# Convolving channel-major projection tiles beside the tile that follows, in a hybrid decoder step

## The chip, the cores and the metric

The kernel runs on one core of a Trainium2 chip. The time is device microseconds of that core, a median over runs. TensorE (PE, with its weight loads as PEld), VectorE (DVE), ScalarE (ACT), GpSimd (POOL) and SyncE (SP) each run one instruction stream in order and wait for each other through semaphores. DMAs are issued from SP, ACT and POOL; a "q" behind an engine's name in a row (SPq) is the engine's issue of one.

## The reference

One layer works on a prompt of 512 tokens and on 8 sequences of 4 new tokens (the sample, 32 rows), model width 2048. Everything starts from one projection; its first 5120 columns belong to the mLSTM mixer (2048 of q and k before the convolution, then 1024 each of v, output gate and group gate), the rest to sparse attention, its indexer and memory attention.

```python
(m_qk, m_v, m_o, m_gate, m_if, a_q, a_k, a_v, a_gate,
 i_q, i_w, i_k, c_q, c_gate) = split_in(rms_norm(x, g_pre) @ w_in)
qk, conv_state = causal_conv(m_qk, zeros, conv_w, conv_b)     # 4 taps over time, per channel, + bias, SiLU
m_out, (C, n, m) = mlstm_mixer(qk, m_v, m_o, m_if, b_if, head_norm, carry0, MLSTM_CHUNK)
```

`causal_conv` also returns the last three rows of `m_qk` (output `p_conv`). The mixer has 4 heads of 256 channels; each uses 256 channels of q and 256 of k. The sample has the same layer with its own states. At the end the three mixers' outputs are gated, joined, multiplied by `w_out`, normed and added to `x`.

## The kernel before

**Stages in order of time.** (1) Input rows are normed and turned, split into a high and a low FP32R part (`x_hi`, `x_lo`); (2) two tiles of memory keys and values; (3) the projection columns from 5120 up, for attention and the indexer; (4) ten tiles of 512 columns, n = `N_B0` to `N_Y0` - 1, which are columns 0 to 5119; the first four hold the 2048 columns that are convolved; (5) memory attention of the sample, with the gates of the mLSTM beside it (`beside_memory`); (6) the four mLSTM heads of the prompt, with the sample's mLSTM beside them (`beside_head`: preparation beside head 0, then 32 pairs of batch and head, 8 in each of heads 1 to 3 and 8 behind); (7) the output projection.

**A tile** (`tensor_tile`, L404 on) goes through 8 chunks of 256 rows of `w_in`. ACT casts a chunk to `w_hi` (L385), POOL subtracts to get `w_lo` (L389), both in two buffers. PE multiplies for each of four blocks of 128 tokens and for the sample rows: the tokens' `x` is the stationary operand and the 512 weight columns stream (L431 to L433; sample L426, L427), so a bank holds tokens by columns. At the tile's end ACT scales each bank by the tokens' `rstd` into `z_tile` (L471) and stores it to DRAM (`z_p`, L476).

**What is hosted.** Between chunks the streams carry pieces of other work, by generators that are stepped at fixed places: PE and ACT twice in a chunk, DVE two prompt steps and one step of `rows` per chunk. During the ten tiles this is the prompt's attention, block of 128 queries after block (`vector_prompt_prep`, L645; `vector_prompt_select`, L1184 to L1200, the scores added up and a top-k; `vector_prompt_attend`, L1275 to L1295), and the sample's sparse attention (physical addresses at L804 to L817, then one row after the other: POOL gathers, DVE multiplies and sums, L906 and L908). The order of the rows of each engine is thus written out in the program. POOL does a tile's `w_lo` and then one row's gather, and that waits until DVE has consumed the row two before.

**The heads.** SP loads for each head five blocks from `z_p`, two heads ahead: head h+2 after head h is through (`sync_mlstm_head`, L1534). q and k must be turned to channels by tokens: for each of 4 blocks of 128 channels of a head, PE turns (L1655, `tensor_conv_turn`), DVE runs four operations over 512 tokens from PSUM (L1667, L1669, `vector_conv`), ACT applies SiLU (L1681, `scalar_conv`). For head 0 this stands alone before the heads; for head h+1 one block stands in each of the four steps of head h. A step of a head is: DVE forms the decay's argument (L1764), ACT takes its exponential (L1849), PE multiplies keys by queries (L1709), DVE combines (L1769). Then PE sums over values (L1722, L1725), forms the new state (L1732, L1737), and DVE norms (L1780 to L1805). A pair of the sample is L2093, L2111, L2116 on PE, L2134 on ACT, L2145 and L2155 on DVE. The sample's preparation begins when SP has loaded its rows (L1921 to L1923; `vector_mlstm_s_prep`, L1965 on).

## Time and profile before

| | |
|---|---|
| median of 3 runs | 1880.14 us (1877.06 to 1888.46) |
| the profiled execution | 1877.01 us |
| its span | 1875.3 us |
| TensorE matmul busy | 1679.8 us (90%) |
| VectorE busy | 814.8 us (43%) |
| ScalarE busy | 569.1 us (30%) |
| GpSimd busy | 673.4 us (36%) |
| mean granted TensorE clock | 0.937 of full |

The profiled execution takes 1.7 us more than its span. Each busy time is a mean over all stages; the stages are read by windows of time. The ten tiles of stage 4 lie from about 567 to 1257 us, memory attention from 1257 to 1325, the heads from there to about 1600. Line numbers in rows are those of the kernel before.

### The profile page before, as it was taken

The page shows a single profiled execution, that of the slowest core. Times are in us where ns is not written, and L with a number is a line of the kernel's source. Part 1 is how long each engine was busy: PE and PEld are TensorE (multiplying, and loading weights), DVE is VectorE, ACT ScalarE, POOL GpSimd, SP SyncE. Part 2 cuts the span into 40 slices and gives each one's busy share as a digit, 9 for nine tenths or more (in the row PEclk, how much of TensorE's full clock was granted, in tenths as well). Part 3 has the DMA queues.
Part 4 walks back from the last instruction along what each step waited for, and adds up shares of the span by engine and source line. Part 5 has one row for each costly group of instructions (what it writes and reads, how often), then busy time and mean ns, then how long its engine had stood idle before and what let it go on. Part 6 is the DMA issues. An engine that isn't in the chain of part 4 may idle for free.

```text
span 1875.3 us, 20980 instructions
## 1 busy us (share of the span) xinstructions
PE 1679.8 (90%) x7801; PEld 1272.0 (68%) x7801; DVE 814.8 (43%) x1319; ACT 569.1 (30%) x876; POOL 673.4 (36%) x448
## 2 busy tenths in 40 slices
PE   6899999999999499998899999987658789799995
PEld 5677775677897376776688778865334455477774
DVE  6400010599929856755632161112465454501113
ACT  5522233222221233233222422224244443312221
POOL 3655531333333166766444444421110111033331
PEclk9999999999999699999999999998667788789997
DMA  6544431233344267766455544437404323542222
GB/s 214 160 134 130 142 101 56 71 105 108 92 120 144 77 196 231 221 197 211 122 154 165 149 134 117 147 125 230 93 29 152 107 68 107 192 160 85 83 78 106
DMA packets 139674, 249.01 MB, mean 133 GB/s; under 512 B 26504, under 2 KB 63308, under 8 KB 136296
## 3 DMA queue, kind: packets, MB, share of 16 engines
q10 hardware_dynamic: 66928, 122.86, 21.0%
q1 hardware_dynamic: 55920, 72.76, 12.2%
q0 software_dynamic: 16736, 52.18, 9.6%
q8 instruction: 58, 0.95, 0.2%
q14 instruction: 32, 0.26, 0.0%
HBM read 204.11 MB, written 43.66 MB: 132 GB/s over the span
## 4 chain that ended last, share of the span: by engine, by line
PE 73%; DVE 13%; DMA 5%; ACT 4%; issue 2%; POOL 1%; ACTq 1%; SPq 0%; DVEq 0%; POOLq 0%
PE acc L431 16%; PE acc L433 16%; PE acc L432 16%; PE acc L426 4%; PE acc L427 4%; PE ps_c L991 3%; PE acc L1722 2%; DVE arena L1669 1%; PE ps_c L2116 1%; PE acc L2111 1%; DMA arena<-z_prompt 1%; PE ps_a L1155 1%; POOL w_lo L389 1%; ACT z_tile L471 1%; PE ps_a L1224 1%
## 5 line engine op out<-in xcount | busy, mean ns | idle before, releaser
L389 POOL TENSOR_TENSOR w_lo<-w_raw,w_hi 128x1024 fp32r<-128x1024 f32 (+1 forms) x200 | 466.7, 2334 | 814.8 <-ACT w_hi L385 814.5
L431 PE MATMUL acc<-w_hi,x_hi 128*128 128x512 f32 (+1 forms) x1472 | 580.4, 394 | 8.8 <-DVE keep L925 5.3
L433 PE MATMUL acc<-w_hi,x_lo 128*128 128x512 f32 (+1 forms) x1472 | 565.9, 384 | 0.0
L432 PE MATMUL acc<-w_lo,x_hi 128*128 128x512 f32 (+1 forms) x1472 | 565.3, 384 | 0.0
L385 ACT CAST w_hi<-w_raw 128x1024 fp32r<-128x1024 f32 (+1 forms) x200 | 204.2, 1021 | 758.3 <-PE acc L427 716.6
L431 PEld LDWEIGHTS acc<-w_hi,x_hi 128*128 128x128 f32 x1472 | 278.8, 189 | 93.9 <-issue 28.0
L433 PEld LDWEIGHTS acc<-w_hi,x_lo 128*128 128x128 f32 x1472 | 278.1, 189 | 55.8
L432 PEld LDWEIGHTS acc<-w_lo,x_hi 128*128 128x128 f32 x1472 | 278.8, 189 | 51.4 <-issue 0.7
L426 PE MATMUL acc<-w_hi,x_hi 128*64 128x512 f32 (+1 forms) x368 | 141.4, 385 | 0.0
L427 PE MATMUL acc<-w_lo,x_hi 128*64 128x512 f32 (+1 forms) x368 | 140.9, 384 | 0.0
L2231 DVE TENSOR_TENSOR arena<-arena (+1 forms) x16 | 14.0, 887 | 176.8 <-ACT arena L464 176.8
L471 ACT ACTIVATE z_tile<-acc,small 128x512 f32<-128x512 f32 (+3 forms) x95 | 63.6, 669 | 48.3 <-PE acc L433 32.1
L881 POOL DMA_INDIRECT arena<-in_cache_attn_k,keep x64 | 67.4, 1054 | 19.5 <-issue 19.5
L795 DVE MAX8 keep<-arena 32x8 f32<-32x2052 f32 x32 | 73.2, 2286 | 1.1
L796 DVE FIND_INDEX8 arena<-keep,arena 32x8 uint32<-32x2052 f32 x32 | 72.9, 2277 | 0.0
L797 DVE MATCH_REPLACE8 arena<-keep,arena 32x2052 f32<-32x2052 f32 x32 | 72.6, 2268 | 0.0
L427 PEld LDWEIGHTS acc<-w_lo,x_hi 128*64 128x64 f32 x368 | 49.5, 134 | 31.5 <-issue 0.2
L657 DVE TENSOR_TENSOR arena<-arena 32x1104 f32<-32x1104 f32 x1 | 1.3, 1297 | 158.3 <-DMA arena<-z_sample 158.3
L881 POOL DMA_INDIRECT arena<-in_cache_attn_v,keep x64 | 62.2, 972 | 14.5 <-issue 11.6
L426 PEld LDWEIGHTS acc<-w_hi,x_hi 128*64 128x64 f32 x368 | 49.5, 135 | 23.6 <-issue 0.2
L991 PEld LDWEIGHTS ps_c<-arena 128*128 128x128 f32 x512 | 62.1, 192 | 4.4
L991 PE MATMUL ps_c<-arena 128*128 128x1 f32 x512 | 58.9, 245 | 0.0
(439 smaller groups left out, 1903.0 us busy)
## 6 DMA issues: line engine op xcount, KB each, us to landing
w_raw<-in_w_in ACTq DMA_DIRECT2D x136, 512.0 KB, 3.7
z_prompt<-z_tile ACTq DMA_DIRECT2D x68, 256.0 KB, 2.5
w_raw<-in_w_out ACTq DMA_DIRECT2D x32, 512.0 KB, 3.6
arena<-z_prompt SPq DMA_DIRECT2D x4, 2088.0 KB, 10.2
w_raw<-in_w_mem_kv ACTq DMA_DIRECT2D x16, 512.0 KB, 4.1
arena<-q_sample POOLq DMA_DIRECT2D x32, 256.0 KB, 4.0
arena<-z_prompt SPq DMA_DIRECT2D x10, 512.0 KB, 7.3
between<-z_prompt SPq DMA_DIRECT2D x10, 512.0 KB, 10.1
```

Of the source, the lines that this page charges most:

```text
L385: nc.scalar.copy(w_hi[:, c % 2, :, 0:w], w_raw[:, c % RAWS, :, 0:w]).then_inc(chunk_hi, 1)
L389: nc.gpsimd.tensor_tensor(out=w_lo[:, c % 2, :, 0:w], in0=w_raw[:, c % RAWS, :, 0:w], in1=w_hi[:, c % 2, :, 0:w].bitcast(F32), op=ALU.subt ...
L426: nc.tensor.matmul(acc[m][0:2 * R, 0:w], xs, wh, start=first, stop=False)
L427: last = nc.tensor.matmul(acc[m][0:2 * R, 0:w], xs, wl, start=False, stop=end)
L431: nc.tensor.matmul(acc[m][:, 0:w], xh, wh, start=first, stop=False)
L432: nc.tensor.matmul(acc[m][:, 0:w], xh, wl, start=False, stop=False)
L433: last = nc.tensor.matmul(acc[m][:, 0:w], xl, wh, start=False, stop=end)
L471: nc.scalar.activation(z_tile[0:rows, m, 0:w], acc[m][0:rows, 0:w], ACT.Copy, scale=rstd(NU_MEM + m, rows)).then_inc(acc_read, 1)
L795: dlink(nc.vector.max(top8, score))
L796: dlink(nc.vector.max_index(sel_idx[:, 8 * i:8 * i + 8], top8, score))
L881: pool.indirect_dma_start(out=got_v[s][:, c, :], out_offset=None, in_=v_rows if values else k_rows, in_offset=bass.IndirectOffsetOnAxis(ap ...
L991: last = nc.tensor.matmul(ps_c[:, PC_O + h * R + r:PC_O + h * R + r + 1], got_v[s][:, c, h * AD:(h + 1) * AD], probs_t[:, c, h, r:r + 1], ...
```

## The change

The four tiles of convolved columns (n = `N_B0` to `N_B0` + 3) are projected channel-major: the weights are the stationary operand and the 512 tokens stream, so that a bank holds 128 channels by 512 tokens. The number and shape of the matmuls stay. ACT copies such a bank to `z_tile` unscaled and starts no store. DVE then does in the first four chunks of the next tile what `vector_conv` now holds: it multiplies by `rstd` along the tokens (a row `rstd_bc` spread over the partitions), keeps the last three tokens in `small`, and runs the four operations, all from SBUF to SBUF. In chunk 6 of that tile ACT applies four SiLUs and stores to a new scratch tensor `qk_prompt` (`late`). The z_tile's rows for the sample go as before.

`rstd_bc` and the coefficients `conv_c` are made at the end of the third stage's first tiles (`tensor_late_consts`, `vector_late_consts`); the coefficients' loads move to the start of the program and their turning out of the gates. Heads load q and k as finished rows from `qk_prompt`, in two DMAs of 512 KB, and the three others as before; their turning, convolution and SiLU are gone. `p_conv` is now stored from `small` in six DMAs whose elements are single FP32 values, 1024 each, ahead of head 0's loads on SP's queue; it was one DRAM to DRAM copy of three rows.

```diff
@@ tensor_tile
+                            if kind == "t":
+                                xh, xl = hi_t[:, k, 0:S], lo_t[:, k, :]
+                                wh, wl = (v[:, c % 2, i, m * P:(m + 1) * P] for v in (w_hi, w_lo))
+                                nc.tensor.matmul(acc[m][:, :], wh, xh, start=first, stop=False)
+                                nc.tensor.matmul(acc[m][:, :], wl, xh, start=False, stop=False)
+                                last = nc.tensor.matmul(acc[m][:, :], wh, xl, start=False, stop=end)
+                                continue
@@ scalar_evacuate
+                if kind == "t" and m < MT:
+                    nc.scalar.copy(z_tile[:, m, :], acc[m][:, :]).then_inc(acc_read, 1)
+                    continue
@@ scalar_tile
+                if c == CH - 2 and late is not None:
+                    late()
@@ new
+        def tensor_late_consts(pe):
+            pe.wait_ge(*at("rstd_spread"))
+            pe.wait_ge(tables_in, 16 * N_TABLES)
+            for m in range(MT):
+                nc.tensor.matmul(ps_c[:, m * P:(m + 1) * P], conv_a[:, m * P:(m + 1) * P], ident[:, :], start=True, stop=True)
+            for k in range(KT):
+                last = nc.tensor.transpose(ps_b[:, k * (CK + 1):(k + 1) * (CK + 1)], conv_nat[:, k * P:(k + 1) * P],
+                                           ident[0:CK + 1, 0:CK + 1])
+            last.then_inc(reached("late_turned"), 1)
...
+        def vector_conv(dve, i, m):
+            k = 4 * i + m
+            dve.wait_ge(acc_read, acc_base(N_B0 + i) + m + 1)
+            dlink(nc.vector.tensor_tensor(out=conv_a, in0=z_tile[:, m, :], in1=rstd_bc, op=ALU.mult))
+            nc.vector.tensor_copy(last_rows(k // 8)[:, k % 8, :], conv_a[:, S - CK + 1:S])
+            out = z_tile[:, m, :]
+            dlink(nc.vector.tensor_scalar(out, conv_a, conv_c[:, k, CK - 1:CK], None, ALU.mult))
+            for j in range(1, CK):
+                ins = nc.vector.scalar_tensor_tensor(out=out[:, j:S], in0=conv_a[:, 0:S - j],
+                                                     scalar=conv_c[:, k, CK - 1 - j:CK - j], in1=out[:, j:S],
+                                                     op0=ALU.mult, op1=ALU.add)
+                if j < CK - 1:
+                    dlink(ins)
+            ins.then_inc(cv_tapped, 1)
+            dve.wait_ge(cv_tapped, k + 1)
+        def scalar_conv(act, i):
+            for m in range(MT):
+                k = 4 * i + m
+                act.wait_ge(cv_tapped, k + 1)
+                nc.scalar.activation(z_tile[:, m, :], z_tile[:, m, :], ACT.Silu, bias=conv_c[:, k, CK:CK + 1]).then_inc(cv_silu, 1)
+            for m in range(MT):
+                k = 4 * i + m
+                act.wait_ge(cv_silu, k + 1)
+                act.dma_start(qk_p[k * P:(k + 1) * P, :], z_tile[:, m, :]).then_inc(z_stored[m], 16)
@@ sync_mlstm_consts
-            sp.dma_start(O["p_conv"].rearrange("l b j c -> (l b j) c"), z_p[S - CK + 1:S, 0:2 * MW]).then_inc(conv_out, 16)
+            sp.wait_ge(cv_tapped, 4 * NCT)
+            for half in range(2):
+                for j in range(CK - 1):
+                    sp.dma_start(O["p_conv"][0, 0, j, half * MW:(half + 1) * MW].rearrange("(k p) -> p k", p=P),
+                                 last_rows(half)[:, :, j], allow_slow_non_contiguous=True).then_inc(conv_out, 16)
@@ sync_mlstm_head
-            for i, c in enumerate((C_QK, C_QK + MW, C_O, C_G, C_V)):
+            for i in range(2):
+                src = qk_p[i * MW + h * MD:i * MW + (h + 1) * MD, :].rearrange("(d p) t -> p d t", p=P)
+                sp.dma_start(qk_t[h % 2][:, i, :, :], src).then_inc(zh_in[h % 2], 16)
+            for i, c in enumerate((C_V, C_O, C_G)):
@@ tensor_mlstm_head, vector_mlstm_head, scalar_mlstm_head: a block of head h+1 no longer stands in each step
-                if h + 1 < H:
-                    tensor_conv_turn(pe, h + 1, i)
-                if h + 1 < H:
-                    vector_conv(dve, h + 1, i)
-                if h + 1 < H:
-                    scalar_conv(act, h + 1, i)
@@ @block.vector, the ten tiles
-            for _ in range(CH * NBT):
+            for i in range(CH * NBT):
                 next(prompt, None)
                 next(rows, None)
                 next(prompt, None)
+                if 0 < i // CH <= NCT and i % CH < MT:
+                    vector_conv(dve, i // CH - 1, i % CH)
@@ @block.vector, before the heads (likewise on PE and ACT)
-            for u in range(4):
-                vector_conv(dve, 0, u)
```

How the order of DVE changes in the fourth of the ten tiles, beside the top-k of the second block of queries (L906 and L908 are one gathered row, L1196 and L1197 one round of the top-k; L979, L981, L1269 and L1270 are the same lines in the changed kernel). Before:

```order
L1196 MAX keep_p<-arena 128x8
L1197 MATCH_REPLACE arena<-keep_p,arena 128x256
L906 TENSOR_TENSOR arena<-arena 128x1024
L908 TENSOR_REDUCE arena<-arena 128x8
L1196 MAX keep_p<-arena 128x8
L1197 MATCH_REPLACE arena<-keep_p,arena 128x256
```

And now:

```order
L979 TENSOR_TENSOR arena<-arena 128x1024
L981 TENSOR_REDUCE arena<-arena 128x8
L1269 MAX keep_p<-arena 128x8
L1270 MATCH_REPLACE arena<-keep_p,arena 128x256
L701 TENSOR_TENSOR arena<-z_tile,head_rows 128x512
L702 COPY small<-arena 128x3
L704 TENSOR_SCALAR z_tile<-arena,conv_cols 128x512
L706 SCALAR_TENSOR_TENSOR z_tile<-arena,conv_cols,z_tile 128x511
L706 SCALAR_TENSOR_TENSOR z_tile<-arena,conv_cols,z_tile 128x510
L706 SCALAR_TENSOR_TENSOR z_tile<-arena,conv_cols,z_tile 128x509
L1269 MAX keep_p<-arena 128x8
L1270 MATCH_REPLACE arena<-keep_p,arena 128x256
```

Six instructions of one block of channels now stand between two rounds of the top-k; the same is inserted in each of the first four chunks of the second to the fifth tile.

The order of DVE in head 1, between its first and its second step (L2145 and L2155 are a pair of the sample, L2163 and L2173 now). Before:

```order
L2145 TENSOR_SCALAR w_raw<-between,keep_m 32x256 x2
L2155 SCALAR_TENSOR_TENSOR mem_kv<-mem_kv,z_tile,acc 128x512
L1667 TENSOR_SCALAR arena<-acc,keep_m 128x512
L1669 SCALAR_TENSOR_TENSOR arena<-acc,keep_m,arena 128x511
L1669 SCALAR_TENSOR_TENSOR arena<-acc,keep_m,arena 128x510
L1669 SCALAR_TENSOR_TENSOR arena<-acc,keep_m,arena 128x509
L2145 TENSOR_SCALAR w_raw<-between,keep_m 32x256
L2155 SCALAR_TENSOR_TENSOR mem_kv<-mem_kv,z_tile,acc 128x512
L1764 TENSOR_SCALAR arena<-ps_b,keep_m 128x384
```

And now:

```order
L2163 TENSOR_SCALAR w_raw<-between,keep_m 32x256 x2
L2173 SCALAR_TENSOR_TENSOR mem_kv<-mem_kv,z_tile,acc 128x512
L2163 TENSOR_SCALAR w_raw<-between,keep_m 32x256
L2173 SCALAR_TENSOR_TENSOR mem_kv<-mem_kv,z_tile,acc 128x512
L1787 TENSOR_SCALAR arena<-ps_b,keep_m 128x384
```

The four operations between the two pairs are gone, in all four steps of heads 0, 1 and 2; head 3 had none.

## Rows read from the trace of the kernel before

**Rows 1.** The page: span and busy time of each engine.
```profile
span 1875.3 us, 20980 instructions
...
PE 1679.8 (90%) x7801; PEld 1272.0 (68%) x7801; DVE 814.8 (43%) x1319; ACT 569.1 (30%) x876; POOL 673.4 (36%) x448
```

**Rows 2.** Chain of waits, heads 0 to 3: start us, us, what.
```profile
1391.10 6.25 PE acc L1722 x20
1414.77 7.69 DMA arena<-z_prompt
1460.95 7.34 PE acc L1722 x20
...
1529.59 7.16 PE acc L1722 x20
...
1580.26 7.42 PE acc L1722 x20
```

**Rows 3.** Busy time by stretch: us, PE, PEld, DVE, ACT, POOL (instructions), PEclk, DMA share, GB/s.
```profile
1391.00:1461.00 70.00, 54.39 (x212) 32.90 (x211) 42.51 (x89) 31.04 (x48) 4.70 (x2) 0.82 0.35 109
...
1530.00:1580.00 50.00, 44.77 (x190) 26.78 (x189) 24.72 (x65) 19.88 (x37) 4.69 (x2) 0.91 0.33 100
```

**Rows 4.** Chain of waits, first convolution to head 0: start us, us, what.
```profile
1325.50 0.76 DVE arena L1667
...
1341.53 2.73 DVE between L1965
...
1357.14 1.06 PE acc L1655 x4
1358.23 0.76 DVE arena L1667
...
1361.36 0.72 ACT between L1681
1362.11 1.28 ACT L1849
```

**Rows 5.** SP in order of time: its issue of the third load for the sample rows.
```profile
1329.39 0.42 SPq L1923 DMA_DIRECT2D keep_p<-const_causal_s  x1
```

**Rows 6.** The DMA view: the same load, KB, us to landing.
```profile
keep_p<-const_causal_s SPq DMA_DIRECT2D x1, 4.0 KB, 10.2
```

**Rows 7.** Busy time by stretch, second to fifth of the ten tiles (columns of Rows 3).
```profile
624.00:699.00 75.00, 61.17 (x279) 48.33 (x279) 47.13 (x99) 26.55 (x50) 32.38 (x25) 0.89 0.47 147
699.00:761.00 62.00, 60.11 (x277) 43.99 (x277) 42.02 (x64) 22.13 (x40) 39.25 (x32) 1.00 0.73 224
761.00:822.00 61.00, 61.00 (x283) 49.03 (x282) 42.32 (x87) 18.20 (x31) 46.71 (x36) 1.00 0.70 209
822.00:891.00 69.00, 62.52 (x287) 47.37 (x287) 35.89 (x63) 23.07 (x41) 40.96 (x33) 0.98 0.68 216
```

**Rows 8.** Groups on DVE, 690:1257: busy us, mean ns of one, idle before.
```profile
L1186 DVE SCALAR_TENSOR_TENSOR arena<-arena,keep_p 128x256 f32<-128x256 f32 x15 | 15.1, 1007 | 5.5 <-ACT arena L1168 5.2
...
L917 DVE TENSOR_TENSOR arena<-arena 128x512 f32<-128x512 f32 x1 | 0.7, 691 | 0.0
```

**Rows 9.** DVE in order of time, third tile: start us, us.
```profile
726.99 0.48 DVE L1186 SCALAR_TENSOR_TENSOR arena<-arena,keep_p 128x256 f32<-128x256 f32 x1
...
730.47 2.96 DVE L1186 SCALAR_TENSOR_TENSOR arena<-arena,keep_p 128x256 f32<-128x256 f32 x2 [0.48 <-ACT arena L1168]
```

**Rows 10.** POOL in order of time, the same stretch.
```profile
730.24 2.39 POOL L389 TENSOR_TENSOR w_lo<-w_raw,w_hi 128x1024 fp32r<-128x1024 f32 x1 [2.32 <-ACT w_hi L385]
```

**Rows 11.** Waits of DVE, 771:797: us in total, times, longest us.
```profile
DVE arena L906 <- issue: 6.2, 3, 2.4
```

**Rows 12.** Waits of PE, 567:891: us in total, times, longest us.
```profile
PE ps_a L1116 <- DVE arena L1089: 22.0, 3, 14.7
```

**Rows 13.** The DMA view, 1325:1328.4: packets, MB, share of 16 engines.
```profile
q1 hardware_dynamic: 200, 0.07, 8.3%
```

**Rows 14.** Chain of waits, the convolution's coefficients turned: start us, us, what.
```profile
1288.64 1.09 PE acc L1553 x16
```

More of the change, by code:

```diff
@@ L58, in hybrid_decoder_step @@
     NBT = C_IF // TN
+    NCT = 2 * MW // TN
     N_Y0 = N_B0 + NBT
@@ L491, in tile_loop, with scalar_tile @@
                 body(n0 + 1)
-        def scalar_tile(act, n, kind, steps=NO_STEPS, often=False):
+        def scalar_tile(act, n, kind, steps=NO_STEPS, often=False, late=None):
             for c in range(1, CH + 1):
@@ L566, in hybrid_decoder_step @@
         gate_s = keep[:, 912:1040]
+        CK = 4
+        conv_nat = place(X_OFF, [2 * MW], CK + 1)
+        conv_a = place(X_OFF + 3112, [S])
+        conv_c = conv_cols[:, :].rearrange("p (k j) -> p k j", j=CK + 1)
+        last_rows = lambda half: small[:, 32 * half:32 * half + 24].rearrange("p (k j) -> p k j", j=CK - 1)
         POOL_PAGES = 2 * CH * IXT
@@ new lines, in vector_late_consts @@
+        def vector_late_consts(dve):
+            dve.wait_ge(rstd_ready, 2)
+            for m in range(MT):
+                last = nc.vector.tensor_copy(conv_a[:, m * P:(m + 1) * P], rstd(NU_MEM + m, P).broadcast_to([P, P]))
+            last.then_inc(reached("rstd_spread"), 1)
+            dve.wait_ge(*at("late_turned"))
+            nc.vector.tensor_copy(rstd_bc, ps_c[:, :])
+            nc.vector.tensor_copy(conv_c, ps_b[:, 0:KT * (CK + 1)].rearrange("p (k j) -> p k j", j=CK + 1)
+                                  ).then_inc(reached("late_copied"), 1)
+            dve.wait_ge(*at("late_copied"))
@@ L1490, in hybrid_decoder_step @@
         assert M0 + 15244 <= AR_N
-        conv_nat = place(M0 + 10252, [2 * MW], CK + 1)
         ifp = place(M0 + 12300, [MT, 2 * H])
@@ L1549, in tensor_mlstm_gates @@
             nc.tensor.transpose(GATES[2][0:H, 2 * R:2 * R + NB], m0_nat, ident[0:NB, 0:NB]).then_inc(g_turned, 1)
-            yield
-            pe.wait_ge(g_copied, 5)
-            for k in range(KT):
-                last = nc.tensor.transpose(GATES[0][:, k * (CK + 1):(k + 1) * (CK + 1)], conv_nat[:, k * P:(k + 1) * P],
-                                           ident[0:CK + 1, 0:CK + 1])
-            last.then_inc(reached("conv_w_t"), 1)
             yield
@@ L1576, in scalar_mlstm_gates @@
             yield
-            act.wait_ge(*at("conv_w_t"))
-            nc.scalar.copy(conv_c, GATES[0][:, 0:KT * (CK + 1)].rearrange("p (k j) -> p k j", j=CK + 1)).then_inc(reached("conv_w_c"), 1)
             act.wait_ge(*at("g_abs"))
@@ L2429, in _ @@
             for n in range(N_B0, N_Y0):
-                scalar_tile(act, n, "b", steps)
+                i = n - N_B0
+                scalar_tile(act, n, "t" if i < NCT else "b", steps,
+                            late=(lambda i=i: scalar_conv(act, i - 1)) if 0 < i <= NCT else None)
             run(steps[0])
@@ L2469, in _ @@
             run(mem_s)
-            for u in range(4):
-                vector_conv(dve, 0, u)
             prep, pairs = vector_mlstm_s_prep(dve), vector_mlstm_s(dve)
@@ L2502, in _ @@
             tensor_gather_out(pe)
-            beside_memory(tensor_mem_s(pe), tensor_mlstm_gates(pe), (4, 6, 9))
-            for u in range(4):
-                tensor_conv_turn(pe, 0, u)
+            beside_memory(tensor_mem_s(pe), tensor_mlstm_gates(pe), (4, 9))
             prep, pairs = tensor_mlstm_s_prep(pe), tensor_mlstm_s(pe)
```

114 lines of the change are left out of this document (40 added, 74 removed).

## The prediction

> **What bounds the kernel now.** I read the page first: PE's matmuls are busy 1679.8 us of a span of 1875.3 [rows 1]. So outside PE's own work only some 195 us can be won, and the question for each stage is what PE waits for. The change touches two stages: the heads, where the convolution leaves, and the ten projection tiles, where it arrives.
>
> *Heads.* The chain of waits passes the start of each head's sums over values (L1722) at 1391.10, 1460.95, 1529.59 and 1580.26 us [rows 2]. The first two intervals, which are head 1 and head 2, take 69.85 and 68.64 us; the third, head 3, takes 50.67. Head 3 carries as many pairs of the sample as the others; what it lacks is the convolution of a next head and the loads of a head two further. The windows say the same: over head 1 DVE is busy 42.5 us, over head 3 24.7, and PE's granted clock is 0.82 against 0.91 [rows 3]. Inside head 1 the chain also takes 7.69 us for a load of head 2's q and k, which PE needs only to turn them [rows 2].
>
> *Tiles.* The second to the fifth of the ten tiles take 75, 62, 61 and 69 us, with DVE busy 47.1, 42.0, 42.3 and 35.9 [rows 7]. The DVE is free for 19 to 33 us in each, but not where one likes: PE, ACT and DVE go through the prompt's attention step by step, and PE already waits 22.0 us for DVE at L1116 [rows 12].
>
> **The change part by part.**
>
> 1. *Heads 1 and 2 lose the convolution.* They become what head 3 is: 69.85 - 50.67 = 19.2 and 68.64 - 50.67 = 18.0, together -37 us. Neither the loads of head h+2 nor the states' loads are then awaited: the loads come when head h ends and are used a head of 50 us later, against some 8 us to land [rows 2]. Bounds: all of it, or only the DVE time of the four blocks, 4 x 4 x 0.76 = 12 us a head [rows 4], so 24 to 37. I take 37, because head 3 is a measured case of the same code, less 1 for the sample's preparation, which now ends just before head 1's first pair: -36.
>
> 2. *Head 0.* Of a block of head 1's convolution the chain carries the turning 1.06, four operations of 0.76 with their gaps (1358.23 to 1361.36, so 3.13), the SiLU 0.72 and the reload of the exponential's table 1.28 [rows 4], in all 6.2 us. Three of the four blocks stand before 1391.10, 18.6 us. Something comes up in their place: a product of keys by queries, which hid under the first block, and the table load for the sample's own SiLU. I put 3.6 on that, half a block, and get -15. Bounds -9 (half hidden) to -18.6.
>
> 3. *Head 0's own four blocks*, 1325.50 to 1341.53, 16.0 us on the chain [rows 4]. Here little is won: behind them stands the sample's L1965, and it needs SP's three loads, issued once memory attention has ended; the last is issued at 1329.39 [rows 5] and lands 10.2 us later [rows 6], at 1339.6. So L1965 moves from 1341.5 to 1339.6: -2. Late next is this load. Bounds 0 to -4.
>
> 4. *The gates beside memory attention* lose the turning of the coefficients, 1.09 us on the chain [rows 14]: -1.
>
> 5. *DVE in the tiles.* One block is a multiplication of 128x512 (L917: 691 ns), a small copy, a multiplication by a scalar and three fused operations. Uncontended I take 0.69 [rows 8], about 0.6 for the copy and the next together, and 3 x 0.76 [rows 4], so 3.6 us. But in this stretch the fused operation on 256 elements takes 1007 ns in the mean [rows 8] where one took 0.48 alone, and two of them 2.96 while POOL's subtraction of 2.39 us, which began at 730.24, ran [rows 9, 10]. Adding the 0.52 to each of five operations gives 6.2. I take 5 us, the middle: 16 blocks, 80 us of DVE.
>
>    What of it reaches PE: in the second tile (attention of the first block of queries, light on DVE) two of four blocks fall in waits, and DVE may be one half chunk, about 4 us, behind before PE stops: 5 us. In the third tile two blocks fall into idle time before the scores; two stand amid them, where a chunk leaves DVE (62 - 42) / 8 = 2.5 us [rows 7]: 2 x (5 - 2.5) = 5. In the fourth tile four blocks, 20 us, stand beside the top-k, where DVE waits only 6.2 us for gathers [rows 11]: 20 - 6.2 - 4 of slack = 9.8. In the fifth, the third block stands before L1089, for which PE waits, and the first delays the end of the attention before it a little, on which the next load hangs: 5 + 1.5 = 6.5, the 1.5 an estimate from a block's 5 us against waits of DVE of some 3.5. The sum is 26 us. Bounds: 8 (all but the fifth tile is slack) to 86, all 80 us and the 6 more on contended operations.
>
>    By the Trainium skill (SBUF — State Buffer, "Who interferes with whom") a VectorE instruction with two inputs in SBUF and a GpSimd instruction that reads SBUF block each other for the whole instruction, and copies and scalar multiplications in the two-port mode do too. The pair of 2.96 us beside a subtraction of 2.39 agrees. It is a rule against this change, whose source moves from PSUM to SBUF; with a whole 2.39 us lost once per block a block would be 6.0 us.
>
> 6. *ACT in the tiles*: four SiLUs of 0.72 with table loads of 1.28 each way [rows 4] are 5.4 us in chunk 6 of four tiles, 21.8 in all. ACT is busy 18 to 27 us in tiles of 61 to 75 [rows 7], and DVE's delay covers most. On PE: +2, bounds 0 to 12. Copying a bank without a store between lets the next tile's first products start sooner, -2 in all, bounds 0 to -4.
>
> 7. *The early constants*: 4 products of 128 columns and 16 small turnings on PE (16 took 1.09 [rows 14]): +2. Clock lost behind PE's new stops: +2, bounds 0 to 8, from 0.89 granted in the tile with the longest stop and 1.00 in those without [rows 7].
>
> 8. *`p_conv`'s six DMAs*: 6144 elements. 200 packets, 72 of them under 512 B, took 8.3% of 16 engines over 3.4 us [rows 13], 23 ns each; so about 6144 x 23 / 16 = 9 us of all engines, between the constants and head 0's loads. SP waits next for memory attention, which ends at 1325.5 [rows 4], some 37 us after the coefficients are turned [rows 14], and head 0's loads are needed only then: covered, 0 on the path, bounds 0 to 9. In the Trainium skill (DMA: Bandwidth & Descriptors, "Rules for kernel authors") a strided last dimension becomes one descriptor per element; no run here shows such a DMA yet.
>
> Sum: -36 - 15 - 2 - 1 = -54 in the heads, and 26 + 2 - 2 + 2 + 2 = +30 in the tiles: -24 on the profiled execution's 1877.0 us, 1853. The median of the runs shown is 3.1 us above the profiled execution; for that I go up by 1: **1854 us**.
>
> **Rivals.**
>
> A. *The tiles swallow the convolution.* DVE is over 19 us idle in each tile [rows 7] and 80 us stand against 99.7 idle; only the fifth tile's term of 6.5 and the fixed 2 stay. Then 1877 - 54 + 9 = 1832. For it: PE is only bound to DVE at a few lines. Against: L1116 shows DVE late already [rows 12].
>
> B. *The heads give back less.* Head 3 has neither loads of a later head nor their load on the DMA engines; with the states' transfers beside them, heads 1 and 2 win only the 12 us of DVE work each (the lower bound of item 1) instead of 18: 12 less, and head 0 its lower bound, 6 less: 1872. Against: head 3, with the same transfers of states.
>
> C. *DVE paces the tiles: slower.* POOL issues a row's gather only when DVE has consumed the row two before, and its next `w_lo` stands behind. If DVE is more than about a chunk and a half behind, PE has no weights: each block of channels then costs PE all its time, in the second to the fifth tile, 16 x 6.2 = 99 less 12 of idle time before loads = 87 instead of 26: 1914. It turns the sign from the point where the tiles lose over 54 us, that is 3.4 us a block. For it: 42 of 61 us are taken in the third and fourth tiles [rows 7], and 20 to 25 come on top.
>
> **Numbers.** My forecast (1838 to 1870) has 0.52, A 0.20, B 0.16, C 0.10, and 0.02 are left for what I haven't thought of. The range from 1831 to 1884 takes in the forecast's own, more than half of A's chance and nearly all of B's, with the 9 us of item 8 and the 12 of item 6 on top of the forecast, and leaves C out. By the skill's rule on the shared port alone (a block of 6.0 us, 16 us of DVE more than I sum) the time would be 1870, the upper end of my forecast's own range. A measurement of this kernel tells about 1% from no change. Under 1861 lie A and two thirds of the forecast: 0.20 + 0.34 = faster 0.54; within 1% the rest of the forecast and most of B, 0.36; slower: C, over 1899, 0.10.
>
> **What would show it.** Heads at about 50 to 52 us apart in the chain; head 0's sums some 35 us behind L1965 instead of 50; the load of the third head's data gone from the chain (1). L1965 still waiting for the sample's load (3). The 16 blocks at about 5 us each in the DVE's order of time, the third and fourth tile longer by 8 to 10 us and PE waiting there for ACT or DVE (5). I am wrong if the five tiles grow by under 15 or over 45 us, or if a head keeps over 55.

## The result: no gain, 0.7% the other way

| | before | changed |
|---|---|---|
| median | 1878.93 us (1873.55 to 1888.46, 6 runs) | 1892.95 us (1886.57 to 1899.66, 6 runs) |
| ratio to before | | 1.0066, 95% interval 1.0046 to 1.0085 |
| the profiled execution | 1877.01 us | 1899.66 us |

The forecast was 1854 us with a range of 1831 to 1884; the time lies above it. The profiled execution of the changed kernel is the slowest of its six; some 5 us of what follows in the tiles, and perhaps as much in memory attention, belong to it alone, and are named. Its page:

```profile
span 1897.8 us, 20879 instructions
...
PE 1671.0 (88%) x7745; PEld 1266.4 (67%) x7745; DVE 845.2 (45%) x1357; ACT 545.0 (29%) x858; POOL 676.8 (36%) x448
...
DMA packets 143860, 249.01 MB, mean 131 GB/s; under 512 B 32741, under 2 KB 65449, under 8 KB 140485
```

PE is busy 9 us less than before [rows 1] in a span 22.5 us longer: PE waits more. The 32741 packets under 512 B were 26504 before, with the same megabytes; this is the first trace of the cause.

**The heads came out as forecast.** Chain of waits of the changed kernel (start us, us, what), the rows that answer to [rows 2]:

```profile
1444.02 5.11 PE acc L1746 x20
...
1501.01 7.34 PE acc L1746 x20
...
1551.95 7.47 PE acc L1746 x20
...
1603.10 7.49 PE acc L1746 x20
```

Head 1 takes 56.99 us, head 2 50.94, head 3 51.15; no load of a head's data is in the chain any more. Behind head 3 nothing changed (294.7 us to the end, 295.1 before).

**Memory attention did not.** The same view between the last tile's sample store and the sample's preparation, beside [rows 4]:

```profile
1294.67 2.87 DMA z_sample<-z_tile
...
1311.11 29.28 DMA between<-in_cache_mem_k
...
1341.83 19.77 DMA between<-in_cache_mem_k
...
1373.38 6.47 DMA w_raw<-in_cache_mem_v
...
1398.07 10.43 DMA keep_p<-const_causal_s
1408.53 2.83 DVE between L1983
```

Two loads of 512 KB of keys stand in the chain with 29.28 and 19.77 us. Before, the stage had one load of keys in its chain, with 8.27 us:

```profile
1257.51 2.90 DMA z_sample<-z_tile
...
1277.50 8.27 DMA w_raw<-in_cache_mem_k
...
1310.74 4.01 DMA between<-in_cache_mem_v
```

I measure the stage from the sample store to SP's issue of its own result (the first store of `mix_sample` from `between`): 68.0 us before, 99.7 now. Two other traces below that hold all six stores, `e5_pool_light` and `e9_no_silu`, have 94.1 and 94.0, so the stage grows by 26 to 32 us.

**The tiles.** Windows of the second to the fifth tile, the answer to [rows 7] (us, PE, PEld, DVE, ACT, POOL busy, clock, DMA share, GB/s):

```profile
631.00:713.00 82.00, 63.59 (x287) 49.32 (x286) 61.24 (x119) 31.24 (x55) 38.31 (x29) 0.92 0.50 152
713.00:781.00 68.00, 63.42 (x280) 46.72 (x279) 63.64 (x97) 24.88 (x44) 42.98 (x33) 0.95 0.65 198
781.00:858.00 77.00, 60.90 (x272) 48.22 (x271) 62.75 (x107) 19.63 (x35) 40.19 (x33) 0.89 0.55 162
858.00:934.00 76.00, 65.20 (x292) 48.72 (x292) 55.44 (x86) 25.36 (x42) 41.67 (x32) 0.93 0.65 206
```

From sample store to sample store they take 82.4, 67.7, 76.7 and 76.3 us, before 75.4, 62.2, 60.0 and 68.7: 36.7 us more. DVE is busy 78 us more in them. Five other traces below have the same four tiles (`e1_no_pconv`, `e2_pconv_turned`, `e7_half`, `e8_packed`, `e11_stores_early`): 296.9 to 298.9 us, which is 30.5 to 32.5 more than before. The third tile's 67.7 us, 62.4 to 63.6 in those five, is this execution's own.

The whole difference of the two spans, by such marks:

| stretch | before | changed | difference | forecast |
|---|---|---|---|---|
| to the end of the first tile | 629.8 | 630.8 | +1.0 | +1 (items 6, 7) |
| second to fifth tile | 266.4 | 303.1 | +36.7 | +29 (items 5 to 7) |
| sixth to tenth tile | 361.4 | 360.8 | -0.6 | 0 |
| memory attention | 68.0 | 99.7 | +31.7 | -1 (item 4), 0 (item 8) |
| to head 0's sums | 65.6 | 49.7 | -15.9 | -17 (items 2, 3) |
| head 1 | 69.9 | 57.0 | -12.9 | -18 (item 1) |
| head 2 | 68.6 | 50.9 | -17.7 | -18 (item 1) |
| head 3 and the rest | 345.8 | 345.8 | +0.1 | 0 |

The heads gave 46 us. The tiles took 37, and memory attention, where nothing was expected, 32.

### The profile page after: what moved, and what is told of

It is laid out like the page before. It is cut to its first block, busy times and chain, and to the rows that moved or that the text cites. A ratio compares the mean times of both kernels' runs of the same rounds, so it can differ in the third digit from the quotient of the medians.

```text
span 1897.8 us, 20879 instructions
## 1 busy us (share of the span) xinstructions
PE 1671.0 (88%) x7745; PEld 1266.4 (67%) x7745; DVE 845.2 (45%) x1357; ACT 545.0 (29%) x858; POOL 676.8 (36%) x448
## 2 busy tenths in 40 slices
DMA packets 143860, 249.01 MB, mean 131 GB/s; under 512 B 32741, under 2 KB 65449, under 8 KB 140485
## 4 chain that ended last, share of the span: by engine, by line
PE 72%; DVE 14%; DMA 7%; ACT 4%; issue 2%; POOL 1%; ACTq 1%; SPq 0%; DVEq 0%; POOLq 0%
PE acc L440 14%; PE acc L442 14%; PE acc L441 14%; PE acc L428 4%; PE acc L429 4%; PE ps_c L1064 3%; DMA between<-in_cache_mem_k 3%; PE acc L2129 2%; PE ps_c L2134 2%; PE acc L1746 1%; DVE z_tile L706 1%; DMA arena<-z_prompt 1%; PE acc L436 1%; PE ps_a L1735 1%; PE acc L437 1%
## 5 line engine op out<-in xcount | busy, mean ns | idle before, releaser
L440 PE MATMUL acc<-w_hi,x_hi 128*128 128x512 f32 (+1 forms) x1216 | 475.6, 391 | 8.5 <-DVE keep L998 5.3
L442 PE MATMUL acc<-w_hi,x_lo 128*128 128x512 f32 (+1 forms) x1216 | 465.0, 382 | 0.0
L441 PE MATMUL acc<-w_lo,x_hi 128*128 128x512 f32 (+1 forms) x1216 | 464.4, 382 | 0.0
L440 PEld LDWEIGHTS acc<-w_hi,x_hi 128*128 128x128 f32 x1216 | 229.9, 189 | 79.8 <-issue 25.4
L442 PEld LDWEIGHTS acc<-w_hi,x_lo 128*128 128x128 f32 x1216 | 229.3, 189 | 45.1
L441 PEld LDWEIGHTS acc<-w_lo,x_hi 128*128 128x128 f32 x1216 | 229.8, 189 | 42.1 <-issue 0.7
L436 PE MATMUL acc<-x_hi,w_hi 128*128 128x512 f32 x256 | 107.1, 418 | 0.2
L437 PE MATMUL acc<-x_hi,w_lo 128*128 128x512 f32 x256 | 102.6, 401 | 0.0
L438 PE MATMUL acc<-x_lo,w_hi 128*128 128x512 f32 x256 | 102.4, 400 | 0.0
L954 POOL DMA_INDIRECT arena<-in_cache_attn_k,keep x64 | 68.6, 1072 | 19.5 <-issue 19.5
L429 PEld LDWEIGHTS acc<-w_lo,x_hi 128*64 128x64 f32 x368 | 49.5, 134 | 31.7 <-issue 0.4
L954 POOL DMA_INDIRECT arena<-in_cache_attn_v,keep x64 | 62.1, 971 | 14.5 <-issue 11.4
```

Of the source, the lines that this page charges most:

```text
L429: last = nc.tensor.matmul(acc[m][0:2 * R, 0:w], xs, wl, start=False, stop=end)
L436: nc.tensor.matmul(acc[m][:, :], wh, xh, start=first, stop=False)
L437: nc.tensor.matmul(acc[m][:, :], wl, xh, start=False, stop=False)
L438: last = nc.tensor.matmul(acc[m][:, :], wh, xl, start=False, stop=end)
L440: nc.tensor.matmul(acc[m][:, 0:w], xh, wh, start=first, stop=False)
L441: nc.tensor.matmul(acc[m][:, 0:w], xh, wl, start=False, stop=False)
```

## The experiments

Two groups: where the 32 us of memory attention come from, and what the tiles pay for. All ratios are to the kernel before on the same chip.

### 1. The small stores of `p_conv`

**Without them.** `e1_no_pconv`:

```diff
-            for half in range(2):
-                for j in range(CK - 1):
-                    sp.dma_start(O["p_conv"]... "(k p) -> p k" ...)
```

> The changed kernel with the six stores of p_conv left out (that output is not written); nothing else differs. Theory S (the single-element stores hold the DMA engines while POOL's loads of cache_mem_k wait for them): the stretch from the sample store of the last tile to the end of memory attention goes from 99.7 back to about 68 us, the loads of cache_mem_k land in 6 to 8 us instead of 18 to 20, and the time is 1893 - 32 = 1861 us. Rival L (the heads' loads, now half of them from qk_prompt, collide with the loads of memory attention, and the stores cost nothing): under 5 us is won, 1888 or more.

Measured: 1862.65 us, ratio 0.9917 (0.9892 to 0.9942). Memory attention takes 70.8 us, keys land in 6.8 us at the median (19.8 with the stores). The stores thus cost 30 us between the medians, 1892.95 and 1862.65, and 28 by the ratios.

**The same edit in the kernel before.** `e4_before_small`:

```diff
-            sp.dma_start(O["p_conv"].rearrange("l b j c -> (l b j) c"), z_p[S - CK + 1:S, 0:2 * MW])
+            for half in range(2):
+                for j in range(CK - 1):
+                    sp.dma_start(O["p_conv"][0, 0, j, half * MW:(half + 1) * MW].rearrange("(k p) -> p k", p=P),
+                                 ident[:, 8 * j:8 * j + 8], allow_slow_non_contiguous=True)
```

> The kernel before with its one store of p_conv (3 rows, DRAM to DRAM) replaced by six stores of 1024 single FP32 elements each from SBUF, at the same place in SP's order; they carry other numbers than p_conv's. Theory S: this one edit brings the loss to the kernel before: memory attention from 67.7 to about 100 us, the time 1879 + 32 = 1911. Rival L: within 5 us of 1879, since the loads of the heads are those of before.

Measured: 1906.45 us, ratio 1.0142 (1.0110 to 1.0174). Chain of waits of this kernel:

```profile
1273.28 26.71 DMA between<-in_cache_mem_k
...
1302.31 19.02 DMA between<-in_cache_mem_k
```

The stage takes 97.8 us, 30 more than before; the whole kernel loses 26, where S said 32. The two rows are those of the changed kernel, in a kernel that shares nothing else with the change. Together the two experiments show the cause, not only its size: theory S holds, L falls. The eight values that one partition gives to one store lie side by side here; it is enough that they are scattered in DRAM.

**How they cost it.** The DMA view of the changed kernel from 1310 to 1335 us, while PE waits for the first of the two loads (queue, kind: packets, MB, share of 16 engines; q0 is POOL's queue, q1 SP's):

```profile
q0 software_dynamic: 203, 0.77, 81.2%
q1 hardware_dynamic: 2452, 0.01, 15.3%
```

And of the kernel before, from 1273 to 1298 us:

```profile
q1 hardware_dynamic: 5202, 5.17, 64.9%
q0 software_dynamic: 1018, 3.71, 40.2%
```

Read the packet counts with the shares (a share of 16 engines over 25 us is a share of 400 engine-microseconds). A small packet on q1 is on record with 15.3% x 400 / 2452 = 25 ns, just what I had reckoned (23). But POOL's packets beside them go from 40.2% x 400 / 1018 = 0.16 us to 81.2% x 400 / 203 = 1.6 us each, ten times longer, and POOL's queue moves 0.77 MB where it moved 3.71. The small element's price does not stand in its own record; it stands in the records of whoever shares the engine.

Nor is it paid while the elements are on record. In these 25 us 2452 small packets went through 16 engines, one in 163 ns each in the mean, but in bursts. From 1315 to 1320 us there are almost none, and POOL's packets take 86.3% x 80 / 40 = 1.7 us all the same:

```profile
q0 software_dynamic: 40, 0.16, 86.3%
q1 hardware_dynamic: 7, 0.00, 0.2%
```

With half of the stores (`e7_half`, below) it is plainer still. Between 1302 and 1307 us 3293 packets under 512 B are on record; from 1312 to 1320 there is none, and POOL's take 63.7% x 128 / 48 = 1.7 us:

```profile
DMA packets 93, 0.29 MB, mean 36 GB/s; under 512 B 0, under 2 KB 0, under 8 KB 93
q0 software_dynamic: 48, 0.20, 63.7%
```

So the elements leave the record early and everything behind them stays slow for many microseconds. Where they are held up meanwhile, the trace doesn't show.

SP itself is held too (its queue in order of time: start, us, what):

```profile
1307.74 26.23 SPq L1596 DMA_DIRECT2D out_p_conv<-small  x6
1334.02 11.17 SPq L1607 DMA_DIRECT2D arena<-qk_prompt  x2
1345.22 14.97 SPq L1611 DMA_DIRECT2D arena<-z_prompt  x3
```

The heads' loads left 26 us late; nobody waited for those. Of the six issues one took 22.5 us (ns min/median/max, first and last start):

```profile
L1596 SPq DMA_DIRECT2D out_p_conv<-small x6: 395/633/22485, 1307.7 to 1333.4; - x6
```

**Count or bytes.** `e7_half` stores only the first half (3 DMAs, 3072 elements). `e8_packed` stores all, each partition's eight values in one piece of 32 B:

```diff
-  O["p_conv"][0, 0, j, half * MW:(half + 1) * MW].rearrange("(k p) -> p k", p=P)
+  O["p_conv"][0, 0, j, half * MW:(half + 1) * MW].rearrange("(p k) -> p k", p=P)
-  last_rows = lambda half: small[:, 32 * half:32 * half + 24].rearrange("p (k j) -> p k j", j=CK - 1)
+  last_rows = lambda half: small[:, 32 * half:32 * half + 24].rearrange("p (j k) -> p k j", j=CK - 1)
```

> The changed kernel with three of the six stores of p_conv (3072 single elements; half of the output isn't written). Theory S in its linear form (each element costs the same): memory attention from the last tile's sample store to its end goes from 99.7 to about 84 us. Rival F (what costs is that SP's fourth to sixth store find a full queue and the heads' loads come late): with three stores nothing stalls and memory attention takes about 68 us. Rival G (a fixed cost): it stays near 100.

> The changed kernel with the six stores of p_conv writing each partition's eight values side by side in DRAM (32 bytes in one piece, 768 pieces instead of 6144 single elements; the values stand in another order than p_conv's). Bytes, stores and their place in SP's order are the same. Theory S by the number of pieces: 32 / 8 = 4 us remain, memory attention takes about 72 us. Rival B (a store of this size from 128 partitions costs by itself, whatever its pieces): about 100.

| pieces | memory attention | time |
|---|---|---|
| 0 (`e1_no_pconv`) | 70.8 us | 1862.65 us |
| 768 of 32 B (`e8_packed`) | 65.5 us | 1853.99 us, one run |
| 3072 of 4 B (`e7_half`) | 90.6 us | 1883.38 us, one run |
| 6144 of 4 B | 99.7 us (94.1 and 94.0 in two other kernels) | 1892.95 us |

Bytes and the number of stores don't decide, the cutting into single values does: B falls by the packed form (65.5 against its 100). Whether it is the number of the pieces or their smallness, no run separates, since the packed form has fewer and larger ones. F falls too: SP issued the three stores in 1.94 us in all, none of them held up, and the stage still took 90.6 us. It is far from linear. The first half costs 20 us and the second 3 to 9, so S's linear form (84) is short by 7, and `e7_half` alone would not speak against G's fixed cost; only together with the packed form, which has all six stores at no cost that shows, does G fall. The packed form is 5 us below the kernel without stores, one profiled execution each, which I don't explain.

**The same stores elsewhere.** `e11_stores_early` issues them in the eighth tile:

```diff
+                if m == MT - 1:
+                    sync_p_conv(sp)      # the wait for cv_tapped and the six stores, taken out of sync_mlstm_consts
                 sync_prompt_out(sp, m)
```

> The changed kernel with the same six stores of 6144 single elements issued in the eighth tile, behind the stores of the last block's keys and values, some 230 us before memory attention. Theory S (the stores cost whoever shares the DMA engines with them): memory attention takes 68 to 71 us; the eighth and ninth tile, whose weights come in 512 KB every 8 us and land in 3.6, see loads of 15 us or more, and grow together by 0 to 15 us, so 1868 to 1883. Rival (the stores are slow by what they stand behind in memory attention, for instance the constants on the same queue): no load of weights is over 7 us, nothing grows, 1865.

Measured: one run of 1871.54 us. Memory attention is at 69.1 us. The eighth tile takes 85.6 us instead of 77.4, and the loads of weights from 1040 to 1120 us (their waits and landing times):

```profile
  ACT w_hi L387: 12.8, 1
...
DMA to landing us min/median/max: 3.6/12.4/29.5
```

3.6 us is what such a load takes alone. So the price moves with the stores and depends on the slack of whoever shares the engines: 8 us here, 32 in memory attention.

**The repair.** `e2_pconv_turned` turns the rows on PE, so that they leave in rows of 512 B:

```diff
+        conv_rows = keep[0:56, 640:768]
@@ tensor_mlstm_gates
+            pe.wait_ge(cv_tapped, 4 * NCT)
+            nc.tensor.transpose(GATES[2][0:56, P:2 * P], small[:, 0:56], ident[:, :])
@@ scalar_mlstm_gates
+            nc.scalar.copy(conv_rows, GATES[2][0:56, P:2 * P]).then_inc(g_copied, 1)
@@ sync, behind sync_mlstm_head(sp, 1)
+                    row = 32 * half + 8 * j
+                    sp.dma_start(O["p_conv"][0, 0, j, half * MW:(half + 1) * MW].rearrange("(k p) -> k p", p=P),
+                                 conv_rows[row:row + 8, :])
```

> The changed kernel with p_conv's last rows turned on PE beside the gates (one transposition of 128x56, one copy on ACT) and stored in six DMAs of 8 rows of 512 B behind the loads of heads 0 and 1. Theory S: 48 packets instead of 6144 cost nothing that can be seen, memory attention takes about 68 us and the time is 1861 to 1863. Rival L: 1888 or more, as without the stores.

(`last_rows` is laid out here with the eight values of one token side by side, as in `e8_packed`.) Measured: 1863.56 us, ratio 0.9919 (0.9888 to 0.9951), memory attention 69.6 us: as S says, 48 rows of 512 B cost nothing that shows.

### 2. What the tiles pay for

**Without DVE's work.** `e3_no_tile_conv` keeps of `vector_conv` only the small copy:

```diff
-            dlink(nc.vector.tensor_tensor(out=conv_a, in0=z_tile[:, m, :], in1=rstd_bc, op=ALU.mult))
-            nc.vector.tensor_copy(last_rows(k // 8)[:, k % 8, :], conv_a[:, S - CK + 1:S])
-            ... (the tensor_scalar and the three scalar_tensor_tensor)
+            ins = nc.vector.tensor_copy(last_rows(k // 8)[:, k % 8, :], z_tile[:, m, S - CK + 1:S])
```

> The changed kernel with five of the six DVE operations of each block of the convolution left out of the tiles; only the copy of three columns stays, with its wait and semaphore. The products, the SiLUs and the stores of q and k stay, of unconvolved data. Theory D (DVE's work in the tiles costs PE the time): the second to the fifth tile go from 82.4, 67.7, 76.7, 76.3 back to about 76, 62, 60, 69 (36 us less), the time is about 1858. Rival A (ACT's SiLUs and stores, the plain evacuation and the early constants carry it): less than 12 us of the 37 are won, and the fourth tile stays over 70.

Measured: one run of 1872.32 us, 14 us above D's number. The four tiles take 81.3, 62.2, 62.0 and 70.6 us, 276.1 together. With DVE's work they take 303.1 in the changed kernel's trace and 297.1 in that of `e1_no_pconv` (82.4, 62.4, 76.1, 76.2); the 6 between those two are mostly the third tile, 67.7 against 62.4, and belong to the one profiled execution. So taking DVE's work away wins 21 us, most of it in the fourth tile, and A falls. But D falls short too: 10 us are left without it, 6 of them in the second tile. There ACT stands (ACT in order of time, this kernel):

```profile
687.17 1.28 ACT L710 ACT_TABLE_LOAD   x1
688.47 1.34 ACT L710 ACTIVATE z_tile<-z_tile,conv_cols 128x512 f32<-128x512 f32 x2
...
690.45 0.94 ACTq L714 DMA_DIRECT2D qk_prompt<-z_tile  x2
691.49 0.37 ACT L1318 COPY arena<-ps_b 128x256 f32<-128x256 f32 x1 [0.45 <-ACT z_tile L710]
691.88 1.28 ACT L1325 ACT_TABLE_LOAD   x1
693.17 0.51 ACT L1325 ACTIVATE arena<-arena,keep_p 128x256 f32<-128x256 f32 x1
```

From 687.17 to 691.49 ACT serves the convolution, and then reloads the exponential's table: 5.6 us ahead of a copy and an exponential for which PE waits. (The expectation of the next run puts the same stop at 7.2 us; these rows give 5.6.) What PE makes of it, and under it the same stretch of the kernel before, whose tile began 1 us earlier (columns as above):

```profile
691.00:701.00 10.00, 7.88 (x32) 5.96 (x33) 5.18 (x8) 3.71 (x7) 2.65 (x3) 0.83 0.66 198
```

```profile
690.00:700.00 10.00, 10.00 (x48) 7.91 (x47) 5.67 (x6) 2.71 (x3) 6.57 (x6) 1.00 0.92 336
```

PE is idle for 2.1 us and is granted less clock, 0.83 over the window: from 694.9 to 697.9 us, behind the stop, a product takes 0.43 us where it took 0.23 ahead of it. The kernel before has PE busy throughout at 1.00.

**Without the SiLUs.** `e9_no_silu`:

```diff
-                nc.scalar.activation(z_tile[:, m, :], z_tile[:, m, :], ACT.Silu, bias=...).then_inc(cv_silu, 1)
-                act.wait_ge(cv_silu, k + 1)
```

> The changed kernel with the sixteen SiLUs of the tiles left out (q and k are stored without it); DVE's convolution, the stores and their place stay. Without DVE's work the second tile still took 81.3 us, against 82.4 with it and 75.4 before: ACT stood 7.2 us in chunk 6 with the table's change, four SiLUs and four stores, ahead of copies and exponentials of the attention. Theory A2 (the second tile's growth is ACT's stop in chunk 6): it goes back to 77 to 78 us, the fourth and fifth move by 2 or less. Rival D2 (either of DVE and ACT alone is enough to make the second tile late): it stays at 81 or 82.

Measured: one run of 1885.82 us; the four tiles take 81.5, 62.3, 76.1 and 74.7 us, 294.6 together. A2 falls, D2 holds: the second tile is late by 6 us with DVE's work alone, by 6 with ACT's alone and by 7 with both. In this kernel the chain runs through DVE without a gap from 679.8 to 695.3 us, a whole block of the convolution among it, where it ran through ACT's stop in the other. The two delays lie side by side, so that taking away one wins next to nothing. Over the four tiles, against the 266.4 us before: 28 us with DVE's work and no SiLU, 10 us with the SiLUs and no DVE's work, 31 us with both. So DVE's work costs 28 us by itself, and the SiLUs 2 to 3 on top of it. (The four stores are in both; no kernel was run without DVE, ACT and stores.)

**Without POOL in the way.** `e5_pool_light` and its partner `e5b_before_pool_light`:

```diff
             for n in range(N_B0, N_Y0):
-                gpsimd_tile(pool, n, gathers)
+                gpsimd_tile(pool, n, gathers, 16 if N_B0 < n <= N_B0 + 4 else TN)   # columns of w_lo that POOL subtracts
```

> The changed kernel with POOL subtracting only 16 of 512 columns of w_lo in the second to the fifth tile (the rest of w_lo is stale, so the products are others); DVE's work is unchanged. Theory P (POOL's subtraction and DVE's operations from SBUF block each other): the 48 fused operations L706 and the 16 multiplications L701 have no member over 1.0 us, a block takes 3.6 instead of 4.9 us, DVE is busy 20 us less in the four tiles and they are at least 8 us shorter. Rival Q (the long ones of 2.9 us come from something else, such as DMA traffic or ACT): blocks stay at about 4.9 us.

> The kernel before with POOL subtracting only 16 of 512 columns of w_lo in the second to the fifth tile (the products are others), the partner of the same edit on the changed kernel, whose four tiles took 78.0, 61.0, 63.9 and 72.5 us. Theory P (without POOL in the way DVE's 57 us of convolution nearly fit): here the four tiles take within 1 us of 75, 61, 60 and 68, so the convolution costs some 11 us instead of 33. Rival: these four tiles get shorter by 10 us or more here too, and the convolution costs as much as with POOL.

DVE's fused operation of the convolution in the changed kernel, and under it with light subtractions (ns min/median/max, first and last start):

```profile
L706 DVE SCALAR_TENSOR_TENSOR z_tile<-arena,conv_cols,z_tile x48: 748/750/3165, 654.3 to 901.0; 128x511 f32<-128x511 f32 x16, 128x510 f32<-128x510 f32 x16, 128x509 f32<-128x509 f32 x16
```

```profile
L706 DVE SCALAR_TENSOR_TENSOR z_tile<-arena,conv_cols,z_tile x48: 748/750/836, 650.3 to 873.3; 128x511 f32<-128x511 f32 x16, 128x510 f32<-128x510 f32 x16, 128x509 f32<-128x509 f32 x16
```

The median is 750 ns in both; the long ones, up to 3165 ns, are gone. A block takes 4.9 us in the changed kernel (77.7 us for 16) and 3.6 here. P holds for the operations. For the tiles: 275.4 us with the convolution (one run of 1860.37 us, which still has the small stores) and 259.4 without (one run of 1875.65), so it costs 16 us where POOL is light and 31 where it is not. About half of the loss in the tiles is thus POOL and DVE in each other's way, the other half the work itself; that is from one trace of each kernel. The partner was to stay within 1 us of before in each tile and did not: its second tile fell from 75.4 to 70.6. DVE is busy 165.0 us in the four tiles before and 145.5 in the partner, so the operations that were there already suffer from POOL too.

**The same work where DVE is idle.** `e6_late_tiles` is `e2_pconv_turned` with the tiles in another order:

```diff
+        CT0 = 5
             if n >= N_B0:
-                return w_in_v, TN * (n - N_B0)
+                j = n - N_B0
+                return w_in_v, TN * (j - CT0 if CT0 <= j < CT0 + 4 else j + 4 if j < CT0 else j)
@@ kinds of tiles, vector_conv's place and wait, late: all by CT0
-                if 0 < i // CH <= NCT and i % CH < MT:
-                    vector_conv(dve, i // CH - 1, i % CH)
+                if CT0 < i // CH <= CT0 + NCT and i % CH < MT:
+                    vector_conv(dve, i // CH - CT0 - 1, i % CH)
```

> The kernel with the turned p_conv (1863.6 us) and, beside that, another order of the ten tiles: columns 2048 to 4607 are projected in the first five tiles, the four tiles of convolved columns are the sixth to the ninth, the last 512 columns the tenth; the convolution and the SiLUs follow in the seventh to the tenth, where DVE is busy 17 of 76, 33 of 77, 18 of 80 and 2 of 60 us. Theory D (the tiles lose because DVE and ACT have no free time where the attention of the prompt needs them): the second to the fifth tile take what they took before (75, 62, 60, 69), the late ones grow by 0 to 2 each, so about 1863.6 - 33 + 4 = 1835 us. Rival W (80 us of DVE from SBUF cost PE the same wherever they stand, by the clock or by POOL's w_lo being held up): the four late tiles grow by 25 to 33, and the time stays at 1855 to 1865.

Measured: 1835.8 us (1831.95 to 1839.9), ratio 0.9756 (0.9728 to 0.9784): it beats both kernels. Windows of its last four tiles:

```profile
969.00:1046.00 77.00, 77.00 (x435) 64.75 (x434) 35.74 (x96) 23.28 (x43) 35.89 (x24) 1.00 0.54 167
1046.00:1123.00 77.00, 77.00 (x404) 58.77 (x403) 41.86 (x73) 26.89 (x42) 36.28 (x24) 1.00 0.43 125
1123.00:1203.00 80.00, 78.69 (x439) 65.18 (x439) 32.44 (x72) 25.83 (x44) 34.77 (x24) 1.00 0.42 124
1203.00:1265.60 62.60, 61.71 (x318) 50.53 (x317) 20.12 (x32) 15.84 (x19) 24.57 (x15) 1.00 0.42 130
```

DVE carries the same 16 blocks here, and PE is busy for 294 of 297 us at full clock. From sample store to sample store the second to the fifth tile take 75.2, 62.1, 60.0 and 68.5 us, as before; the sixth to the tenth 365.7 against 361.4. The convolution costs 4 us at most instead of 31, since 2.6 of the 4 are in the sixth tile, where none of it stands. W falls. POOL is not what makes the difference: a block takes 3.9 us here, and one fused operation 2.77. The order has a small price elsewhere: the first tile ends at 634.0 us, 3 us later than in the changed kernel.

`e10_one_earlier` sets `CT0 = 4`:

> As the kernel with the late tiles (1835.8 us), with the tiles of convolved columns one place earlier, the fifth to the eighth, so that the convolution follows in the sixth to the ninth; DVE is busy 39 of 67 us in the sixth, which the late order does not use, and the tenth is left free. Theory D (a tile pays when DVE is short of time where PE waits for it): the sixth grows by 4 to 8 us, the tenth falls from 62.9 to 60.2, in sum 1838 to 1841. Rival: within 2 us of 1836, since 20 us fit into 28 us of idle DVE.

Measured: 1839.41 us, ratio 0.9799 (0.9778 to 0.9820); the sixth tile takes 73.5 us (69.3 in the late order), the tenth 60.2 (62.9). Both are as D says. The tiles bear it out and not the totals, since the two orders' intervals overlap.

## Why the prediction was wrong

**The step that failed is item 8**, "covered, 0 on the path, bounds 0 to 9". Measured: +31.7 us in the profiled execution, and 30 of the 39 by which the median missed, since the same kernel without these stores has a median of 1862.65 us. Two things in it were wrong. The price: 23 ns per element was the busy time on record, and 25 ns is what the elements show; but it is not in their own records that they cost. The packets of the queue beside them took ten times as long, and went on doing so while no element was on record. The cover: I asked who waits for SP's next loads, and that was right, nobody did. I did not ask who else uses the 16 engines in that stretch: POOL's loads of keys, on which PE waits chunk by chunk. The page of the Trainium skill that I cited (DMA: Bandwidth & Descriptors, "Rules for kernel authors") gives the one descriptor per element, and the runs agree: the change added 6237 packets under 512 B for 6144 elements.

Without item 8's stores the kernel lies inside the forecast's own 1838 to 1870, and not by errors that cancel: its trace (`e1_no_pconv`) is 15 us under the one before where I had forecast 24, with 2 to 3 us missing in the tiles, 4 in memory attention and 3 in the heads.

**Item 5 had the mechanism, the block and the sum right, and the split wrong.** A block was put at 5 us and took 4.9. On PE I summed 26 us. Measured are 21 (what is won when DVE's work goes and ACT's stays) to 28 (what it costs with the SiLUs gone). By tile, in `e9_no_silu` against before:

| tile | forecast | measured |
|---|---|---|
| second | 5 | 6.1 |
| third | 5 | 0.1 |
| fourth | 9.8 | 16.1 |
| fifth | 6.5 | 6.0 |

That the sum fits although the third and the fourth tile miss by 5 and 6 us is luck. Waits of PE in the fourth tile of the changed kernel (781 to 858 us), where before it had none:

```profile
PE ps_a L1297 <- DVE arena L1361: 16.0, 1, 16.0
```

I had credited 6.2 us of idle time and 4 of slack against four blocks of 5; nothing of it was left when PE came to L1297.

**Item 6 holds as it was meant**: +2 on top of DVE's delay forecast, 2 to 3 measured (297.1 us with the SiLUs, 294.6 without). By itself ACT's stop of 5.6 us in chunk 6 is as late for PE as DVE's blocks are: without DVE's work about 10 us are left.

**The rule of the Trainium skill on SBUF** (SBUF — State Buffer, "Who interferes with whom") was applied to too few operations. With it I put a block at 6.0 us against my 5, and the block is 4.9; but the contention falls on the other operations too. DVE is busy 243 us in the four tiles with POOL's full subtractions and 202 with the light ones, 165.0 and 145.5 in the kernel before: POOL's subtractions cost DVE 20 us before and 41 now. That is as the rule says, and so is the longest fused operation: 3.17 us, which is one of 0.75 and a whole subtraction of 2.4. PE loses 31 us to the convolution with the full subtractions and 16 with the light ones.

**The heads were right.** Head 0 and the sample's load: -17 forecast, -15.9 measured, with L1983 again behind SP's last load (10.43 us), item 3 to the point, and head 0's sums 35.5 us behind it where I had said some 35. Heads 1 and 2: -36 forecast, -30.6 measured. The 5 us short are in head 1, and are clock: from 1460 to 1480 us, with PE busy nine tenths of the time,

```profile
1460.00:1480.00 20.00, 18.14 (x46) 8.76 (x45) 6.41 (x14) 6.15 (x13) 0.00 (x0) 0.57 0.69 223
```

the granted clock is near the lower of its two levels; the four products of a pair (L2129) take 2.00 us there and 1.06 in the next head. By the letter this met a sign that I had set for being wrong, "a head keeps over 55"; yet without such a stretch the head is the 51 us of head 3. Eight of the ten other kernels with this change have such a stretch in head 1 or head 2 (head 2 of `e1_no_pconv`: 54.2 us), two have none (`e5_pool_light`, `e8_packed`: all three heads 50.6 to 51.5). What PE did before that decides it, I could not tell from them. Head 3 before, my model, was without.

**The rivals.** C, "DVE paces the tiles", named the side on which the time fell, but not the reason: the tiles lost 37 us, not 87, and in the four tiles' waits of PE there is none for POOL's `w_lo`. A and B came out neither. None of the four cases had the DMA engines in it.

## What to carry to other kernels

Price a DMA by its pieces, not by its bytes, and not by the busy time of its own packets: ask which loads share the engines in those microseconds and the 20 behind them, and who waits for them. A tail of a few kilobytes that lies across partitions is turned on PE first. And when work moves off a crowded stage, choose the receiving stage by where its engine is idle and PE does not wait for it: the same 16 blocks cost 31 us in the second to the fifth tile and at most 4 in the seventh to the tenth.

## What the runs showed of the hardware

- Beside stores of single FP32 values from SBUF to DRAM, packets of about 4 KB of another queue took 1.6 us instead of 0.16. The elements' own packets are on record with 25 ns, in bursts; the others stayed at 1.7 us in stretches of 5 and 8 us with almost none or none of them on record. Pieces of 32 B, an eighth as many, showed no cost.
- SP's issue of such a store took up to 22.5 us (`L1596`, the changed kernel).
- A fused operation of DVE from SBUF, 750 ns alone, took up to 3.2 us beside POOL's subtraction of 2.4 us, and never over 0.84 when that was short.
